# RWKV chunk inverse: products of (I+P) with [P-I, X], with the odd half of the pairs in the neighbouring column quarter and another PSUM bank

## The chip, the cores and the metric

The kernel runs on one core of one Trainium2 chip. The metric is device time in microseconds. Everything is float32.

## The reference, cut to what matters

One encoder layer over 1024 + 512 tokens of width 1024: RMSNorm, one projection into an RWKV-7 group (8 heads of 64, two directions) and an HGRN2 group, output projection, a mixture of 32 experts, a final norm. The change touches only the RWKV scan:

```python
def step(S, inp):
    r_t, w_t, k_t, v_t, kk_t, b_t = inp
    sa = jnp.einsum('dbhvk,dbhk->dbhv', S, -kk_t)
    S = S * w_t[..., None, :] + sa[..., None] * b_t[..., None, :] + v_t[..., None] * k_t[..., None, :]
    y_t = jnp.einsum('dbhvk,dbhk->dbhv', S, r_t)
    return S, y_t
```

The kernel computes it in chunks of 32 tokens. Inside a chunk the tokens depend on each other through a strictly triangular 32x32 matrix M, one for each head and direction, so 16 of them in each chunk. The chunk needs X = (I-M)^-1 = (I+M)(I+M^2)(I+M^4)(I+M^8)(I+M^16).

## The kernel before, in words

The stage is `mix_rwkv_project_hgrn`. It goes over 48 chunks (50 turns of the loop, since the work on a chunk is spread over three turns: `a = c+2`, `b = c+1`, `c`). Between the pieces of the scan, TensorE computes the HGRN columns of the input projection (`project`, L1202: 54 units of 8 matmuls of 128x512, shared out as 8 or 9 a turn). All orders are written out by hand: each engine has its own loop over the same turns and waits on marks (`Marks`) that other engines set.

The 16 matrices of a chunk lie as 4 partition quarters (`quad[q]`, 32 partitions each) times 4 pairs (`j`). TensorE works here on tiles: a matmul with 32 rows and 32 columns uses the part of the array given by the partition quarter that it reads (row quarter) and the one that it writes (column quarter). A float32 matmul shows as two records in the trace, so 16 matmuls are 32 records. In the text a block is such a set of 16 matmuls:

- right, L1246: the right-hand side from `sm` and `vz`, then L1250 from the state; mark R.
- I2 (`power(ps_b, ..., 2)`, L1231).
- solve, L1259 (X applied to `rs`), then L1262, the output from the state; mark UO.
- scores, L1221, then one projection matmul.
- grow, L1271 and L1275; mark MO.
- I3 (L1231), two projection matmuls, I0 (L1229), three projection matmuls (two in the later turns), I4 (L1234), I1 (L1231). L1231 is one line for I1, I2 and I3.

In L1229, L1231, L1234 and L1259 the matmul of quarter q reads quarter q and writes quarter q, for all pairs, so a block uses four tiles of the array, four times each. L1246 also uses four. L1250 and L1262 (`by_turn`) use eight tiles, each of which has 64 rows and 32 columns, and L1275 has four of that same shape.

VectorE's `grow` (L1439 to L1443) follows each I block: add P X to X, copy the new P out of PSUM (L1441), transpose it as the next stationary operand `pw` (L1443). The first transpose is L1544, the first X (M + I) is L1545, the last add into `xt` is L1556. Before L1544 in each turn VectorE does `grown` (L1536, waits for MO) and `state` (L1539); `masked` (L1431) makes `sm` from the scores. `scans` (L1456 to L1470) and `scaled` are for HGRN. `ps_a` (chunk a) and `ps_b` (chunk b) are one PSUM bank each.

## Time and profile before

| | us |
|---|---|
| median of 3 runs | 2321.32 (2316.4 to 2321.55) |
| profiled execution, its own time | 2317.24 |
| its span | 2315.7 |
| this stage's steady part, 508 to 1211 | 703.00 |

The span is the time between the first and the last record of the profiled execution. The stage is one of several that follow one another; the norm and the RWKV projection lie ahead of it, the HGRN scan, the output projection and the experts behind it. In a timeline row the first number is the start in us from the span's start, the second the time from the first start to the last end of the merged records, then engine, line, operation, operands, shape, count. "Idle before" stands in brackets. Since matmuls are pipelined, the time that a block costs TensorE is read from its start to the next block's start, not from the second number.

### The profile page before, as it was taken

To read this page: it belongs to the slowest core of one execution; us is meant where nothing else is said; L and a number is where in the kernel's file an instruction comes from. 1 tells how busy PE (TensorE), PEld (TensorE's weight loads), DVE (VectorE), ACT (ScalarE), POOL (GpSimd) and SP (SyncE) were. 2 spreads that over 40 slices of the span, in tenths; PEclk is the share of its full clock that TensorE was granted. 3 is DMA by queue.
4 is the path that set the end of the run, shared out by engine and by line. 5 is a ranking of instruction groups with operands and counts; after the bars stand their busy time and mean duration, and the time that the engine had idled before them with its cause. 6 is when DMAs were issued, how large, how long until landed. Compare 5 with 4: busy or idle time off the path is not lost. (4 is left out here: it accounts for less than half of the span.)

```text
span 2315.7 us, 64509 instructions
## 1 busy us (share of the span) xinstructions
PE 2215.1 (96%) x28004; PEld 1453.8 (63%) x28004; DVE 1032.3 (45%) x2221; ACT 717.5 (31%) x1446; POOL 407.9 (18%) x506
## 2 busy tenths in 40 slices
PE   7999999999999999999997999998999999999996
PEld 4444445445555555555556766756888888888884
DVE  3336767833654654644656765655211111111114
ACT  4224545623454543543642322222000000000003
POOL 1012222310000000000002120013524333233231
PEclk9999999999999999999998999998999999999998
DMA  4103444443333333333338754262999999999997
GB/s 144 37 23 128 153 147 137 167 113 93 94 105 88 91 103 94 94 104 89 84 107 258 233 169 132 97 236 70 363 381 335 357 364 328 354 357 335 353 335 293
DMA packets 359966, 436.66 MB, mean 189 GB/s; under 512 B 164994, under 2 KB 296198, under 8 KB 351536
## 3 DMA queue, kind: packets, MB, share of 16 engines
q1 hardware_dynamic: 343232, 397.94, 50.5%
q0 software_dynamic: 14384, 35.19, 6.0%
q8 instruction: 192, 3.15, 0.6%
q10 hardware_dynamic: 2112, 0.01, 0.1%
q14 instruction: 46, 0.38, 0.1%
HBM read 329.84 MB, written 104.50 MB: 188 GB/s over the span
## 5 line engine op out<-in xcount | busy, mean ns | idle before, releaser
L1202 PE MATMUL h_pp<-hT,r_wcol 128*128 128x512 f32 x832 | 414.0, 620 | 3.3 <-ACT h_iraw L1317 3.3
L2925 PEld LDWEIGHTS e_ps_gu<-e_xT,e_wu 128*128 128x128 f32 x2048 | 233.6, 192 | 14.3 <-issue 14.3
L2925 PE MATMUL e_ps_gu<-e_xT,e_wg 128*128 128x128 f32 x2048 | 235.2, 276 | 0.0
L2925 PE MATMUL e_ps_gu<-e_xT,e_wu 128*128 128x128 f32 x2048 | 233.8, 275 | 0.0
L2925 PEld LDWEIGHTS e_ps_gu<-e_xT,e_wg 128*128 128x128 f32 x2048 | 232.5, 193 | 0.4 <-DVE e_xT L3043 0.4
L2934 PE MATMUL e_ps_y<-e_wd,e_hid 128*128 128x512 f32 x512 | 225.1, 592 | 0.8 <-DVE e_hid L3097 0.8
L1202 PEld LDWEIGHTS h_pp<-hT,r_wcol 128*128 128x128 f32 x832 | 141.8, 190 | 124.6 <-issue 109.4
L522 PE MATMUL h_pp<-hT,r_wcol 128*128 128x512 f32 x480 | 209.1, 593 | 1.3 <-DVE hT L794 1.3
L3050 DVE TENSOR_SCALAR e_y<-e_ps_y,e_row 128x512 f32<-128x512 f32 x31 | 23.3, 750 | 325.0 <-PE e_ps_y L2934 325.0
L2934 PEld LDWEIGHTS e_ps_y<-e_wd,e_hid 128*128 128x128 f32 x512 | 94.8, 190 | 108.8 <-issue 107.1
L522 PEld LDWEIGHTS h_pp<-hT,r_wcol 128*128 128x128 f32 x480 | 90.3, 191 | 109.7 <-issue 108.1
L2989 ACT ACTIVATE e_silu<-e_ps_gu 128x512 f32<-128x512 f32 x31 | 18.5, 597 | 410.3 <-PE e_ps_gu L2925 396.6
L2718 POOL DMA_INDIRECT e_x<-h,e_idx x128 | 124.6, 973 | 55.6 <-issue 29.5
L2286 PE MATMUL o_ps_out<-o_wout,y 128*128 128x512 f32 x288 | 129.4, 594 | 4.0 <-DVE y L2520 4.0
L2041 POOL MEMSET g_mask<- 128x256 f32 x1 | 0.3, 312 | 735.3 <-POOLq L1058 735.3
L1379 ACT ACTIVATE m_v<-m_ps_x 32x256 f32<-32x256 f32 x192 | 71.9, 374 | 147.0 <-PE m_ps_x L1262 145.3
L3057 DVE TENSOR_TENSOR e_hid<-e_ps_gu,e_silu 128x512 f32<-128x512 f32 x31 | 21.4, 691 | 204.7 <-PE e_ps_gu L2925 204.7
L776 POOL TENSOR_TENSOR r_spans<-r_spans 128x512 f32<-128x512 f32 x24 | 42.0, 1768 | 370.6 <-DVE r_spans L866 370.6
L522 PE MATMUL r_pp<-hT,r_wcol 128*128 128x512 f32 x240 | 105.4, 592 | 0.0
L2286 PEld LDWEIGHTS o_ps_out<-o_wout,y 128*128 128x128 f32 x288 | 52.2, 190 | 58.6 <-issue 58.6
L522 PEld LDWEIGHTS r_pp<-hT,r_wcol 128*128 128x128 f32 x240 | 45.4, 190 | 56.4 <-issue 56.4
L2985 ACT ACTIVATE e_y<-e_ps_y,e_row 128x512 f32<-128x512 f32 x31 | 21.3, 688 | 184.0 <-PE e_ps_y L2934 184.0
(428 smaller groups left out, 3398.3 us busy)
## 6 DMA issues: line engine op xcount, KB each, us to landing
e_wg<-in_moe_w_gate_dram SPq DMA_DIRECT2D x32, 2048.0 KB
e_wu<-in_moe_w_up_dram SPq DMA_DIRECT2D x32, 2048.0 KB
e_wd<-in_moe_w_down_dram SPq DMA_DIRECT2D x32, 2048.0 KB
r_wcol<-in_w_in_dram SPq DMA_DIRECT2D x35, 512.0 KB, 4.7
ar<-r_ar SPq DMA_DIRECT2D x24, 512.0 KB, 2.7
kb<-r_kb SPq DMA_DIRECT2D x24, 512.0 KB, 2.8
m_ar<-ar SPq DMA_DIRECT2D x48, 256.0 KB, 4.7
m_kb<-kb SPq DMA_DIRECT2D x48, 256.0 KB, 3.5
```

The costliest lines, as they stand in the source:

```text
L522: last = nc.tensor.matmul(pp[k % SPANS][:], wcol[q][:, c], self.hT[:, c, s * SPAN:(s + 1) * SPAN], start=c == 0, stop=c == KT - 1)
L776: nc.gpsimd.tensor_tensor(gx[d][:], gi[d][:], sg[d][:], ALU.subtract).then_inc(*pool_aux.inc(f"gx{d}"))
L1202: last = nc.tensor.matmul(pp[n % 2][:], wcol[(k + 2) % 3][:, c], self.hT[:, c, span(s)], start=c == 0, stop=c == KT - 1)
L1379: last = nc.scalar.activation(out, ps_ru[quad[q]], ACT.Copy)
L2286: last = nc.tensor.matmul(ps_out[:, h * SPAN:(h + 1) * SPAN], y[:, k, tile(FINISHED[n])], wout[:, k, h * SPAN:(h + 1) * SPAN], start=k == ...
L2718: self.nc.gpsimd.indirect_dma_start(self.e_x[u][:, g], None, self.h2.rearrange("t (q e) -> (t q) e", q=4), bass.IndirectOffsetOnAxis(ap=se ...
L2925: last = nc.tensor.matmul(ps[:, q * P:(q + 1) * P], w[u][:, c, q * P:(q + 1) * P], xT[u][:, c * P:(c + 1) * P], start=c == 0, stop=c == KT ...
L2934: last = nc.tensor.matmul(ps_y[:, n * 512:(n + 1) * 512], hid[u][:, q * P:(q + 1) * P], wd[u][:, q, n * 512:(n + 1) * 512], start=q == 0, ...
L2985: return nc.scalar.activation(y[u][:, 0:512], ps_y[:, 0:512], ACT.Copy, scale=gate[u])
L2989: made = nc.scalar.activation(silu[:], ps_g, ACT.Silu)
L3050: return nc.vector.tensor_scalar(y[u][:, 512:], ps_y[:, 512:], gate[u], None, ALU.mult)
L3057: made = nc.vector.tensor_tensor(hid[u][:], ps_u, silu[:], ALU.mult)
```

## The change

X is kept in PSUM's own sum: with (I+P) as the stationary operand and [P-I, X] as the moving one, a single matmul gives [P^2-I, X+PX]. The first block multiplies M with [M, I]. VectorE adds I (or 2I) to the left half and writes that into a spare part of the same PSUM tile (S), copies both halves into `px` (N), and transposes the spare part out of PSUM (turn). The separate add into X goes, as do X0 and `xt`. For pairs 2 and 3 the matmuls write the neighbouring column quarter (`q ^ 1`) and, as `ps_p` is two banks, the other bank; pairs go in the order 0, 2, 1, 3. The columns of `ps_ru` for w = 1 are exchanged in the same way. As chunks a and b now share `ps_p`, I0, I4 and I1 get one wait more, and one projection matmul stands between I4 and I1.

```diff
-            m0 = sb("m_m0", [P, PAIRS, CH])
+            m0 = sb("m_m0", [P, PAIRS, 2 * CH])
-            xt = [sb(f"m_xt{u}", [P, PAIRS, CH]) for u in range(2)]
-            eye = sb("m_eye", [P, CH])
+            eyes = sb("m_eyes", [P, 3 * CH])
-            ps_a = psum("a", [P, PAIRS, P])
-            ps_b = psum("b", [P, PAIRS, P])
+            ps_p = psum("p", [P, PAIRS, 2 * P])
+            ps_a = ps_b = ps_p
...
-                        nc.gpsimd.affine_select(out=eye[r], in_=eye[r], compare_op=ALU.not_equal, fill=1.0, base=0,
-                                                pattern=[[-1, CH]], channel_multiplier=1).then_inc(filled, 1)
+                        for part, value in enumerate((-1.0, 1.0, 2.0)):
+                            e = eyes[r, part * CH:(part + 1) * CH]
+                            nc.gpsimd.affine_select(out=e, in_=e, compare_op=ALU.not_equal, fill=value, base=0,
+                                                    pattern=[[-1, CH]], channel_multiplier=1).then_inc(filled, 1)
...
                     def power(ps, u, i):
-                        for j in range(PAIRS):
-                            for q in quad:
-                                if i == 0:
-                                    last = nc.tensor.matmul(ps[q, j, 0:CH], pw[u][q, j], m0[q, j], start=True, stop=True)
-                                elif i < 4:
-                                    last = nc.tensor.matmul(ps[q, j, 0:2 * CH], pw[u][q, j], px[u][q, j], start=True,
-                                                            stop=True)
+                        for j in (0, 2, 1, 3):
+                            for q in range(P // CH):
+                                r, o = quad[q], quad[q ^ (j // 2)]
+                                if i < 4:
+                                    last = nc.tensor.matmul(ps[o, j, 0:2 * CH], pw[u][r, j], px[u][r, j] if i else m0[r, j],
+                                                            start=True, stop=True)
                                 else:
-                                    last = nc.tensor.matmul(ps[q, j, CH:2 * CH], pw[u][q, j], px[u][q, j, CH:],
+                                    last = nc.tensor.matmul(ps[o, j, CH:2 * CH], pw[u][r, j], px[u][r, j, CH:],
                                                             start=True, stop=True)
...
-                            nc.tensor.matmul(ps_ru[quad[2 * k + d], w, i], sm[c % RING][r, g, 0:CH], vz[c % 2][r, g],
+                            nc.tensor.matmul(ps_ru[quad[(2 * k + d) ^ w], w, i], sm[c % RING][r, g, 0:CH], vz[c % 2][r, g],
...
-                        for j in range(PAIRS):
-                            for q in quad:
-                                nc.tensor.matmul(ps_ru[q, j % 2, j // 2], xt[c % 2][q, j], rs[q, j], start=True, stop=True)
+                        for j in (0, 2, 1, 3):
+                            for q in range(P // CH):
+                                r = quad[q ^ (j // 2)]
+                                nc.tensor.matmul(ps_ru[quad[q], j // 2, j % 2], px[c % 2][r, j, CH:], rs[r, j], start=True,
+                                                 stop=True)
...
                         if has_a:
-                            self.waits(eng, dve_a.at("P0", a))
+                            self.waits(eng, dve_a.at("P0", a), dve_b.at("turn4", b) if has_b else None)
                             power(ps_a, a % 2, 0).then_inc(*pe_a.inc("I0"))
-                        project(it, 6, 9)
+                        project(it, 6, 8)
                         if has_b:
-                            self.waits(eng, dve_b.at("turn4", b))
+                            self.waits(eng, dve_b.at("turn4", b), dve_a.at("turn1", a) if has_a else None)
                             power(ps_b, b % 2, 4).then_inc(*pe_b.inc("I4"))
+                        project(it, 8, 9)
                         if has_a:
-                            self.waits(eng, dve_a.at("turn1", a))
+                            self.waits(eng, dve_a.at("turn1", a), dve_b.at("X4", b) if has_b else None)
                             power(ps_a, a % 2, 1).then_inc(*pe_a.inc("I1"))
...
                     def grow(marks, ps, b, i):
 
                         u = b % 2
-                        if i > 1:
-                            nc.vector.tensor_tensor(px[u][:, :, CH:], px[u][:, :, CH:], ps[:, :, CH:2 * CH], ALU.add
-                                                    ).then_inc(*marks.inc(f"X{i - 1}"))
-                        nc.vector.tensor_copy(px[u][:, :, 0:CH], ps[:, :, 0:CH]).then_inc(*marks.inc(f"P{i}"))
-                        self.waits(eng, marks.at(f"P{i}", b))
-                        nc.vector.transpose(pw[u][:], px[u][:, :, 0:CH]).then_inc(*marks.inc(f"turn{i}"))
+                        each = lambda lo, n: eyes[:, lo * CH:(lo + n) * CH].unsqueeze(1).broadcast_to((P, PAIRS, n * CH))
+                        spare = ps[:, :, 2 * CH:3 * CH]
+                        nc.vector.tensor_tensor(spare, ps[:, :, 0:CH], each(1 if i == 1 else 2, 1), ALU.add
+                                                ).then_inc(*marks.inc(f"S{i}"))
+                        if i == 1:
+                            nc.vector.tensor_tensor(px[u][:], ps[:, :, 0:2 * CH], each(0, 2), ALU.add
+                                                    ).then_inc(*marks.inc(f"N{i}"))
+                        elif i < 4:
+                            nc.vector.tensor_copy(px[u][:], ps[:, :, 0:2 * CH]).then_inc(*marks.inc(f"N{i}"))
+                        else:
+                            nc.vector.tensor_copy(px[u][:, :, CH:], ps[:, :, CH:2 * CH]).then_inc(*marks.inc(f"N{i}"))
+                        self.waits(eng, marks.at(f"S{i}", b))
+                        nc.vector.transpose(pw[u][:], spare).then_inc(*marks.inc(f"turn{i}"))
...
-                            nc.vector.transpose(pw[a % 2][:], m0[:]).then_inc(*dve_a.inc("P0"))
-                            nc.vector.tensor_tensor(px[a % 2][:, :, CH:], m0[:],
-                                                    eye[:].unsqueeze(1).broadcast_to((P, PAIRS, CH)), ALU.add
-                                                    ).then_inc(*dve_a.inc("X0"))
+                            nc.vector.transpose(pw[a % 2][:], m0[:, :, 0:CH]).then_inc(*dve_a.inc("P0"))
...
-                            nc.vector.tensor_tensor(xt[b % 2][:], px[b % 2][:, :, CH:], ps_b[:, :, CH:2 * CH], ALU.add
-                                                    ).then_inc(*dve_b.inc("X4"))
+                            nc.vector.tensor_copy(px[b % 2][:, :, CH:], ps_b[:, :, CH:2 * CH]).then_inc(*dve_b.inc("X4"))
```

ScalarE's copies into `m0` and `rs` only take the pairs in another order.

## Rows read from the trace of the kernel before

**Rows 1.** The page, part 1: busy time, share of the span, instructions of each engine.
```profile
PE 2215.1 (96%) x28004; PEld 1453.8 (63%) x28004; DVE 1032.3 (45%) x2221; ACT 717.5 (31%) x1446; POOL 407.9 (18%) x506
```

**Rows 2.** Windows, steady part: length; PE, PEld, DVE, ACT, POOL busy; PEclk; DMA; GB/s.
```profile
508.00:1211.00 703.00, 685.57 (x18878) 401.27 (x18872) 368.51 (x1042) 323.19 (x738) 0.00 (x0) 1.00 0.37 94
```

**Rows 3.** Lines of the steady part, two groups of one shape: count, busy, mean, idle before.
```profile
L1275 PE MATMUL m_ps_x<-m_v,m_sm 64*32 64x64 f32 x1504 | 33.1, 220 | 0.6 <-issue 0.6
...
L1262 PE MATMUL m_ps_x<-m_state,m_ar 64*32 64x64 f32 x1504 | 22.9, 222 | 1.8 <-issue 1.8
```

**Rows 4.** Timeline of one turn, TensorE's matmul rows: start, extent, engine, line, count.
```profile
803.25 0.67 PE L1275 MATMUL m_ps_x<-m_v,m_sm 64*32 64x64 f32 x32
...
803.86 0.65 PE L1231 MATMUL m_ps_b<-m_px,m_pw 32*32 32x64 f32 x32
...
804.44 1.98 PE L1202 MATMUL h_pp<-hT,r_wcol 128*128 128x512 f32 x4
...
806.35 0.45 PE L1229 MATMUL m_ps_a<-m_m,m_pw 32*32 32x32 f32 x32
...
806.74 2.84 PE L1202 MATMUL h_pp<-hT,r_wcol 128*128 128x512 f32 x6
...
809.51 0.45 PE L1234 MATMUL m_ps_b<-m_px,m_pw 32*32 32x32 f32 x32
...
809.78 0.65 PE L1231 MATMUL m_ps_a<-m_px,m_pw 32*32 32x64 f32 x31
...
810.24 0.64 PE L1246 MATMUL m_ps_x<-m_v,m_sm 32*32 32x64 f32 x30
...
810.80 0.45 PE L1250 MATMUL m_ps_x<-m_state,m_ar 64*32 64x64 f32 x32
...
813.10 0.65 PE L1231 MATMUL m_ps_b<-m_px,m_pw 32*32 32x64 f32 x32
...
813.57 0.62 PE L1259 MATMUL m_ps_x<-m_rs,m_xt 32*32 32x64 f32 x32
...
814.13 0.45 PE L1262 MATMUL m_ps_x<-m_state,m_ar 64*32 64x64 f32 x32
...
814.51 0.81 PE L1221 MATMUL m_ps_s<-m_ar,m_kb 64*64 64x128 f32 x7
```

**Rows 5.** The same turn, VectorE's rows between MO and the end.
```profile
804.01 0.69 DVE L1536 TENSOR_TENSOR m_grown<-m_ps_x,m_state 128x512 f32<-128x512 f32 x1 [0.83 <-PE m_ps_x L1275]
...
805.34 0.30 DVE L1544 STREAM_TRANSPOSE m_pw<-m_m 128x128 f32<-128x128 f32 x1
...
805.57 0.25 DVE L1545 TENSOR_TENSOR m_px<-m_m,m_eye 128x128 f32<-128x128 f32 x1
805.74 0.28 DVE L1439 TENSOR_TENSOR m_px<-m_px,m_ps_b 128x128 f32<-128x128 f32 x1
805.93 0.28 DVE L1441 COPY m_px<-m_ps_b 128x128 f32<-128x128 f32 x1
806.25 0.31 DVE L1443 STREAM_TRANSPOSE m_pw<-m_px 128x128 f32<-128x128 f32 x1
...
807.21 0.31 DVE L1443 STREAM_TRANSPOSE m_pw<-m_px 128x128 f32<-128x128 f32 x1
...
810.04 0.29 DVE L1556 TENSOR_TENSOR m_xt<-m_px,m_ps_b 128x128 f32<-128x128 f32 x1 [2.52 <-PE m_ps_b L1234]
```

**Rows 6.** Waits of the steady part: engine, line, what was waited for, total us, times, longest.
```profile
PE m_ps_s L1221 <- issue: 3.6, 6, 1.2
```

**Rows 7.** DMA queues of the steady part: packets, MB, share of 16 engines' time.
```profile
q8 instruction: 149, 2.44, 1.5%
```

**Rows 8.** Timeline, a turn with an HGRN scan in it, VectorE's L1536.
```profile
1163.19 0.69 DVE L1536 TENSOR_TENSOR m_grown<-m_ps_x,m_state 128x512 f32<-128x512 f32 x1 [0.36 <-PE m_ps_x L1275]
```

**Rows 9.** Start of the stage: the last constant on GpSimd, the first mask on VectorE.
```profile
487.28 0.69 POOL L1076 TENSOR_SCALAR_AFFINE_SELECT m_mask<-m_mask 32x32 f32<-32x32 f32 x4
...
490.36 0.80 DVE L1431 TENSOR_TENSOR m_sm<-m_ps_s,m_mask 128x256 f32<-128x256 f32 x2 [1.44 <-PE m_ps_s L1221]
```

More of the change, by code:

```diff
@@ L967, in mix_rwkv_project_hgrn @@
             lb0, lb1, lb, olb, nolb = (sb("h_" + n, [P, 2, PAIRS]) for n in ("lb0", "lb1", "lb", "olb", "nolb"))
-            sb("h_below", [P, 92])
+            sb("h_below", [P, 156])
             self.first = kq_first, k3_first, k2_first = self.first_chunk(sb("h_first", [P, 3 * D + SPAN]))
@@ L993, in mix_rwkv_project_hgrn @@
             act_c = Marks(self.sem("m_act_back"), "r u O")
-            dve_a = Marks(self.sem("m_dve_first"), "mask0 mask1 P0 X0 P1 turn1 X1 P2 turn2")
-            dve_b = Marks(self.sem("m_dve_last"), "X2 P3 turn3 X3 P4 turn4 X4")
+            dve_a = Marks(self.sem("m_dve_first"), "mask0 mask1 P0 S1 N1 turn1 S2 N2 turn2")
+            dve_b = Marks(self.sem("m_dve_last"), "S3 N3 turn3 S4 N4 turn4 X4")
             dve_c = Marks(self.sem("m_dve_back"), "grown state")
@@ L1015, in mix_rwkv_project_hgrn @@
             dve_q = Marks(self.sem("h_dve_q"), "Q0 K0 Q1 K1 Q2 K2")
-            FILLED = 3 + 5 * (P // CH) + 3
+            FILLED = 3 + 7 * (P // CH) + 3
             V_LOADS = 16 * 8
@@ L1061, in _ @@
                     nc.gpsimd.memset(mask[:], 1.0).then_inc(filled, 1)
-                    nc.gpsimd.memset(eye[:], 0.0).then_inc(filled, 1)
+                    nc.gpsimd.memset(eyes[:], 0.0).then_inc(filled, 1)
                     nc.gpsimd.memset(state[0][:], 0.0).then_inc(filled, 1)
@@ L1249, in right @@
                             g = 4 * d + 2 * i + w
-                            last = nc.tensor.matmul(ps_ru[quad[2 * (h ^ w) + d], w, i], ar[c % RING][heads[h], g, 0:CH],
+                            last = nc.tensor.matmul(ps_ru[quad[(2 * (h ^ w) + d) ^ w], w, i], ar[c % RING][heads[h], g, 0:CH],
                                                     state[c % 2][heads[h], g], start=False, stop=True,
@@ L1369, in _ @@
                             self.waits(eng, pe_c.at("R", c))
-                            nc.scalar.activation(rs[:].rearrange("p (i w) v -> p w i v", w=2), ps_ru, ACT.Copy
+                            nc.scalar.activation(rs[:].rearrange("p (w i) v -> p w i v", w=2), ps_ru, ACT.Copy
                                                  ).then_inc(*act_c.inc("r"))
@@ L1388, in _ @@
                                 d = q % 2
-                                last = nc.scalar.activation(m0[quad[q]], sm[a % RING][quad[q], d * PAIRS:(d + 1) * PAIRS, 0:CH],
-                                                            ACT.Copy)
+                                last = nc.scalar.activation(
+                                    m0[quad[q], :, 0:CH].rearrange("p (w i) n -> p w i n", w=2),
+                                    sm[a % RING][quad[q], d * PAIRS:(d + 1) * PAIRS, 0:CH].rearrange("p (i w) n -> p w i n", w=2),
+                                    ACT.Copy)
                             last.then_inc(*act_a.inc("m0"))
@@ L1426, in _ @@
                     eng.wait_ge(filled, FILLED)
-                    eng.wait_ge(cleared, 1 + 2 * RING)
+                    nc.vector.tensor_copy(m0[:, :, CH:], eyes[:, CH:2 * CH].unsqueeze(1).broadcast_to((P, PAIRS, CH))
+                                          ).then_inc(cleared, 1)
+                    eng.wait_ge(cleared, 2 + 2 * RING)
                     by_dir = lambda ap: ap.rearrange("p (d i) n -> p d i n", d=2)
```

## The prediction

> **What bounds the kernel now.** I read the page first. TensorE is busy for 96% of the span [rows 1]; the other engines for less than half. A reader should then leave the whole-kernel share alone and ask the stage. The windows view gives, for the 703.0 us between 508 and 1211 us, a busy TensorE of 685.6 us at a granted clock of 1.00 (2.4 GHz), VectorE 368.5 and ScalarE 323.2 [rows 2]. So TensorE's order sets the pace of the 48 chunks, one turn of the loop each, and what matters is how long each block holds TensorE, plus the places where it would have to wait. The kernel's last stage, where the chain of waits ends, isn't touched; what this stage gives back is passed on whole, because all engines leave it together.
>
> The timeline of one turn shows how regular it is [rows 4]. From start to next start: I3 0.58 (803.86 to 804.44), two projection matmuls 1.91, I0 0.38, three projection matmuls 2.77 (these are six records), I4 0.27, I1 0.46, L1246 0.56, I2 0.47, solve 0.56, L1262 0.38, L1275 0.61. The reader is to compare blocks with the same count of records (32) and the same 64 moving columns: L1275 0.61 against L1262 0.38. These two even have the same tile shape, 64 rows by 32 columns. Over the whole steady part it is 33.1 against 22.9 us busy [rows 3], 10.2 us in 47 blocks, 0.22 us a block. The code says what differs: L1275 goes round four tiles of the array, L1262 round eight. Per tile, then, a block is eight passes in a row with four tiles, four passes with eight tiles. I2, which is followed by a block of the same shape with no switch, gives the length of a pass: 0.47/8 = 0.058 us.
>
> **The change part by part.**
>
> *The eight-tile blocks.* By the code, L1246, I0 to I4 and solve now go round eight tiles (quarter q to q, then q to its neighbour, in another bank), as L1262 does today. No row shows eight tiles of 32 rows; the nearest are the 64-row ones. Bounds for one block of 64 columns: nothing saved (if 32-row tiles in one row quarter don't overlap), 0.23 us saved (0.61 - 0.38). I take what lies close to the upper end, because L1262 has four tiles in each row half and they overlap: I2 goes from 0.47 to 0.47 - 4 x 0.056 = 0.25; L1246 from 0.56 and solve from 0.56 to 0.37, a shade under L1262's 0.38, since both are followed by a change of tile shape as it is. Saved on TensorE: I2 0.22, L1246 0.19, solve 0.19, together 0.60 us a turn. I3 would save 0.20 as well, but see the next step.
>
> *I3 and the new wait of I0.* In front of I0 stands now "turn4 of chunk b". Today VectorE, released by MO, does L1536 at 804.01, the state, the transpose L1544 at 805.34, X0 at 805.57, the add 805.74, the copy 805.93 and the transpose of turn4 at 806.25 to 806.56 [rows 5]; I0 starts at 806.35 without waiting for the last one. In the changed order X0 falls away: S4 starts at 805.57, N4 at 805.76 (the present spacing of 0.19), turn4 at about 805.96, since S4 (0.29 long, like the present adds) ends at 805.86, and it ends at about 806.28. With some 0.06 us for the signal I0 starts at 806.34, where it starts today. TensorE would be there at 806.35 - 0.20 = 806.15. So I3's gain turns into a wait of about 0.2 us for VectorE, and MO to I0 stays as long as it is. The forms "add from PSUM into PSUM" and "transpose out of PSUM" have no row. Bounds: as their SBUF twins (0.25 to 0.31), or later by the 0.13 us that today's dependent pair shows over independent ones (0.32 against 0.19 between starts) plus as much again for the PSUM side, which puts I0 0.2 us later; I take 0.0 to 0.05 later. Behind the waiting I0 are the projection matmuls, I4 and I1, thus everything; ScalarE's next unit only follows.
>
> *I0 with 64 instead of 32 columns.* Four tiles at 32 columns cost 0.38 with the shape switch; eight tiles at 64 columns with the switch cost 0.38 (L1262). Nothing.
>
> *I4, the projection between, I1.* Today three projections, I4 and I1 are 2.77 + 0.27 + 0.46 = 3.50 us. Then: two projections 1.91, I4 with eight tiles and a shape switch behind it 0.35 (today I0, with as many columns and four tiles, has 0.38; an eight-tile block of 64 columns has 0.38 as well, so little is won by more tiles on a block of 32), one projection 1.06 (as 2.77 - 1.91 is 0.86 and two switches bring 0.20), I1 0.25. That is 3.57: 0.07 us lost to the two extra switches, in place of 0.21 won on I1. Bounds 0.0 to 0.15 lost.
>
> *The waits of I4 and I1.* turn1 starts at 807.21 and ends 1.17 us after I0's start [rows 5]. N1 is wider (256 elements, about 0.40 by L1431's 0.80 for two of that width [rows 9], 0.12 more than now), and I4 comes 2.3 us after I0: 0.9 us to spare. X4 starts 0.53 us after I4's start and lasts 0.29; I1 comes 1.4 us after I4's start: 0.5 to spare. Both waits are free while VectorE isn't behind.
>
> *VectorE in all.* An instruction goes (X0), three copies grow by about 0.12, so its load is as it was, 52% of the stage [rows 2]. But in the turns with an HGRN scan its work is near the edge: L1536 had waited for MO for 0.36 us only [rows 8], against 0.83 in the other turn [rows 5]. The path from I1 through the scans to L1536 gets 0.6 us shorter on TensorE and not on VectorE, so in about 8 turns (one for each of the 8 scans) L1536 comes some 0.25 us late, 0.6 - 0.36: 2 us.
>
> *Constants.* Eight more small selects on GpSimd at 0.2 us: the last ends at 487.97 today, its first reader starts at 490.36 [rows 9]. 1.6 us fit into 2.4. The VectorE copy of I into `m0` lies there too. Nothing.
>
> *Instruction loading.* TensorE's instructions come in 149 loads in this part [rows 7], one per 4.7 us, and some blocks of short matmuls show holes put down to "issue", in L1221 3.6 us in 6 holes, the longest 1.2 [rows 6]; that is the largest of seven such groups, so all of them stay under 25 us. The count of instructions stays, the blocks get shorter, so a hole can grow by what the blocks before it lost (up to 0.4 us), while the projection put between I4 and I1 gives the loading more time. I take +1 us; from -3 to +10.
>
> *The sum.* -0.60 + 0.07 = -0.53 us a turn; 48 turns make -25.4 us; +2 for the scans and +1 for the loading leave -22.4 us. From the profiled execution (span 2315.7, own time 2317.2) that gives 2294.8. The median of the three runs is 4.1 us above the profiled execution, so in the terms of that median the time is 2321.3 - 22.4 = 2299.
>
> *A rule that speaks against it.* L1250 and L1262 have four column tiles in each row half, and their 32 records take 0.38 us, against 0.61 for four tiles [rows 3, 4]. The Trainium skill (TensorE: Matmul & The Clock Gate, Part 3: Packing small matmuls) says that a weight load overlaps matmuls in flight only when the row group differs. By that rule the tiles q to q and q to its neighbour, which read the same row quarter, would not overlap, and the change would cost time (first rival). The trace disagrees for 64-row tiles; no row shows 32-row ones.
>
> **The rivals.**
>
> 1. *Eight tiles don't overlap (slower).* Place: every I block, L1246, solve. Then nothing is saved, I0 pays for its wider columns (0.58 as I3, against 0.38: +0.20), and the split of I4 and I1 costs 1.91 + 0.41 + 1.06 + 0.47 = 3.85 against 3.50: +0.35. 0.55 x 48 = +26 us: 2348. It decides when a block wins less than 0.55/5 = 0.11 us, half of what I take, since five blocks count (I3's gain is hidden). For it: no row with 32-row tiles. Against it: L1262. Chance 0.06.
> 2. *VectorE's chain to turn4 is longer, or instruction holes grow.* Each 0.1 us on the chain from MO to turn4 is 4.8 us. At +0.2 us it takes 9.6 us, and +8 us of holes come to much the same: 2308. For it: two forms without a row, holes that already lie in the short blocks. Against it: all PSUM forms of this size last 0.28 to 0.29, like the SBUF ones plus 0.03. Chance 0.25.
> 3. *turn4 doesn't hold I0 up.* If N4 overlapped more, I3's 0.2 us would come as well: 9.6 us more, 2289. Against it: L1544 starts 1.33 us after L1536 [rows 5], both wide instructions before it stay, and three instructions follow it. Chance 0.10.
> 4. *No difference.* A combination in which the late turns with scans and the holes take most of it: 2318. Chance 0.07.
>
> **How the numbers follow.** The forecast has 0.52. Its own range is 2293 to 2305. The range for 8 in 10 takes in rival 2 and rival 3 with their bounds: 2285 to 2312. About 0.3% (7 us) is what a measurement can tell from no change. Faster by more: 0.52 + 0.25 + 0.10 = 0.87; within it 0.07 (rival 4); slower 0.06 (rival 1).
>
> **What would show it.** After the change L1246, L1259 and the I blocks with 64 columns should have extents near 0.45, as L1262 has now, not 0.65, and the rows for four against eight tiles in the lines view should be equal; TensorE should show a wait for VectorE's transpose out of PSUM ahead of I0, about 0.2 us, nearly every turn; MO to I0 should stay 2.64 to 2.7 us; a turn with 16 projection records should take about 0.53 us less, so that the stage ends some 22 us earlier; I4 and I1 should start without waiting. It is wrong if blocks keep 0.65 (rival 1), if I0 comes later after MO than today (rival 2), or if the holes put down to "issue" grow past 25 us.

## The result, and the profile after

The changed kernel takes 2336.9 us (median of 8 runs, 2332.4 to 2345.6), the kernel before 2321.4 us in the same series (8 runs): ratio 1.0074, 95% interval 1.0061 to 1.0086. It is 15.5 us slower where 22 us faster was forecast. The time is lost in the stage forecast to gain: the first matmul of the next stage starts at 1239.68 us in place of 1223.28, and what follows is as long as before (1093.2 against 1092.4 us).

The page of the changed kernel, part 1, and the windows view of the same 703 us as in [rows 2] (same columns):

```profile
PE 2207.0 (95%) x28004; PEld 1419.6 (61%) x28004; DVE 1033.4 (44%) x2222; ACT 718.5 (31%) x1446; POOL 409.0 (18%) x514
```

```profile
508.00:1211.00 703.00, 660.27 (x18386) 358.38 (x18376) 364.16 (x1024) 320.34 (x730) 0.00 (x0) 1.00 0.35 91
```

Three things are to be seen here. The clock is the same (1.00), TensorE is busy for 25 us less than in [rows 2], and yet it gets through 492 records fewer in the same time. So it is idle longer, and what fills the idle time is the question. The timeline of one turn of the changed kernel, TensorE's matmul rows (start, extent, then as in [rows 4]):

```profile
900.44 0.67 PE L1277 MATMUL m_ps_x<-m_v,m_sm 64*32 64x64 f32 x32
901.04 0.45 PE L1231 MATMUL m_ps_p<-m_px,m_pw 32*32 32x64 f32 x32
901.42 1.98 PE L1203 MATMUL h_pp<-hT,r_wcol 128*128 128x512 f32 x4
903.57 0.46 PE L1231 MATMUL m_ps_p<-m_m,m_pw 32*32 32x64 f32 x32 [0.16 <-DVE m_pw L1457]
903.96 1.98 PE L1203 MATMUL h_pp<-hT,r_wcol 128*128 128x512 f32 x4
905.87 0.35 PE L1234 MATMUL m_ps_p<-m_px,m_pw 32*32 32x32 f32 x32
906.15 1.12 PE L1203 MATMUL h_pp<-hT,r_wcol 128*128 128x512 f32 x2
907.21 0.45 PE L1231 MATMUL m_ps_p<-m_px,m_pw 32*32 32x64 f32 x32
907.53 0.53 PE L1246 MATMUL m_ps_x<-m_v,m_sm 32*32 32x64 f32 x32
908.00 0.45 PE L1250 MATMUL m_ps_x<-m_state,m_ar 64*32 64x64 f32 x32
908.38 1.98 PE L1203 MATMUL h_pp<-hT,r_wcol 128*128 128x512 f32 x4
910.29 0.45 PE L1231 MATMUL m_ps_p<-m_px,m_pw 32*32 32x64 f32 x32
910.56 0.57 PE L1260 MATMUL m_ps_x<-m_rs,m_px 32*32 32x64 f32 x30
911.80 0.29 PE L1260 MATMUL m_ps_x<-m_rs,m_px 32*32 32x64 f32 x2 [0.67 <-issue]
912.02 0.46 PE L1264 MATMUL m_ps_x<-m_state,m_ar 64*32 64x64 f32 x32
```

Against [rows 4]: I3 takes 0.38 (901.04 to 901.42) in place of 0.58, I2 0.27 in place of 0.47. L1246, right behind I1, takes 0.47, and the solve, right behind I2, is broken off after 30 of its 32 records; in a turn without such a gap it takes 0.52:

```profile
818.32 0.59 PE L1260 MATMUL m_ps_x<-m_rs,m_px 32*32 32x64 f32 x32
818.84 0.31 PE L1264 MATMUL m_ps_x<-m_state,m_ar 64*32 64x64 f32 x6
820.58 0.44 PE L1264 MATMUL m_ps_x<-m_state,m_ar 64*32 64x64 f32 x26 [1.43 <-issue]
```

Such gaps, put down to "issue" (TensorE waited for nothing that the profile shows), are where the time went. The waits view of the changed kernel, 508 to 1230 us (columns as in [rows 6]), the largest groups of the short blocks' matmuls, and the wait of I0 (first and sixth row):

```profile
PEld m_ps_p L1231 <- DVE m_pw L1558: 36.6, 39, 1.3
...
PE m_ps_s L1222 <- issue: 8.4, 9, 1.6
...
PE m_ps_x L1264 <- issue: 7.5, 8, 1.4
...
PE m_ps_x L1277 <- issue: 6.6, 7, 1.2
...
PE m_ps_x L1260 <- issue: 4.5, 6, 1.2
...
PE m_ps_p L1231 <- DVE m_pw L1457: 3.9, 20, 0.5
PE m_ps_x L1246 <- issue: 3.7, 6, 0.9
```

All "issue" rows of the short blocks' matmuls add up to 35.9 us, before to 16.3 us; L1222 has 8.4 us against 3.6 [rows 6]. Where I write "gaps" below I count them from the records themselves: two consecutive matmul records of one short block that start more than 0.18 us apart, between 508 and 1225 us. Before there are 27, together 18 us, after 60, together 50 us. With the gaps taken out, a turn is some 0.3 us shorter than before: 15 us gained, 32 us given away.

What the gaps have in common can be read from the order of the records. Each matmul record stands for two TensorE instructions (a weight load and a matmul), and in both kernels every gap lies at the same place modulo 256 TensorE instructions, so some 127 records from the next possible one. The queue that brings in instructions shows the same step (the changed kernel, 508 to 1230 us, columns as in [rows 7]):

```profile
q8 instruction: 149, 2.44, 1.4%
```

2.44 MB in 149 loads is 16 KB a load, and some 38,000 TensorE instructions in 149 loads are 256 a load. That the gaps lie in short blocks says little by itself, since only 8 or 9 of the some 150 steps between 508 and 1225 us fall in a projection; one of these, at 523.5 us in the changed kernel, shows a pause too (0.88 us between two starts where 0.43 or 0.53 is usual). How deep a step falls in a row of short blocks counts: of those in the first short block behind a projection 13 of 57 have a gap, in the second 22 of 41, in the third 18 of 30, deeper 10 of 11 (before: 6 of 48, 7 of 34, 9 of 32, 8 of 28; counted with a gap between two blocks taken in).

The gaps can also be set against the times of these loads. The load ahead of the gap shown above (TensorE stands from 910.92 to 911.80) runs from 909.30 to 910.43, and the next one begins at 913.41. The DMA view of the changed kernel for 909.2 to 910.5 and for 913.3 to 914.5 us has one load each, for the time between them none:

```profile
q8 instruction: 1, 0.02, 5.4%
...
q8 instruction: 1, 0.02, 5.0%
```

So the gap ends 1.37 us after the end of a load. It is the same nearly everywhere: 57 of the 60 gaps of the changed kernel and all 27 of the one before end 1.1 to 1.7 us after the end of a load (median 1.4), and the other three are among the shortest (0.22 to 0.26 us). Of the short blocks' records in general only some 14% start that far behind a load. Between each two of the 256-instruction steps exactly one load ends at least 1.15 us ahead of the second step, in both kernels, and after a gap the next load never starts earlier than 1.04 us behind it. From load to load it is at least 3.2 us. A gap is thus TensorE standing at the end of its 256 instructions until the next ones are in.

### The profile page after: what moved, and what is told of

Same layout as the page of the kernel before. It is cut to its first block and busy times, and to the rows that moved or that the text cites. A ratio compares the mean times of both kernels' runs of the same rounds, so it can differ in the third digit from the quotient of the medians.

```text
span 2332.9 us, 64667 instructions
## 1 busy us (share of the span) xinstructions
PE 2207.0 (95%) x28004; PEld 1419.6 (61%) x28004; DVE 1033.4 (44%) x2222; ACT 718.5 (31%) x1446; POOL 409.0 (18%) x514
## 3 DMA queue, kind: packets, MB, share of 16 engines
q8 instruction: 192, 3.15, 0.6%
## 5 line engine op out<-in xcount | busy, mean ns | idle before, releaser
L1203 PE MATMUL h_pp<-hT,r_wcol 128*128 128x512 f32 x832 | 426.3, 626 | 3.7 <-ACT h_iraw L1320 3.3
L522 PE MATMUL h_pp<-hT,r_wcol 128*128 128x512 f32 x480 | 211.1, 597 | 1.3 <-DVE hT L794 1.3
L1447 DVE TENSOR_TENSOR m_ps_p<-m_ps_p,m_eyes 128x128 f32<-128x128 f32 x192 | 55.9, 291 | 150.7 <-PE m_ps_p L1231 150.7
L1231 PEld LDWEIGHTS m_ps_p<-m_px,m_pw 32*32 32x32 f32 x4608 | 42.9, 104 | 78.6 <-issue 74.0
```

What stands on the lines that cost most here:

```text
L522: last = nc.tensor.matmul(pp[k % SPANS][:], wcol[q][:, c], self.hT[:, c, s * SPAN:(s + 1) * SPAN], start=c == 0, stop=c == KT - 1)
L1203: last = nc.tensor.matmul(pp[n % 2][:], wcol[(k + 2) % 3][:, c], self.hT[:, c, span(s)], start=c == 0, stop=c == KT - 1)
L1231: last = nc.tensor.matmul(ps[o, j, 0:2 * CH], pw[u][r, j], px[u][r, j] if i else m0[r, j], start=True, stop=True)
L1447: nc.vector.tensor_tensor(spare, ps[:, :, 0:CH], each(1 if i == 1 else 2, 1), ALU.add).then_inc(*marks.inc(f"S{i}"))
```

## The experiments

Each ran beside the kernel before (medians 2320.9 to 2322.5 us in the five series). Labels that begin with a_ are edits of the changed kernel, with b_ of the one before. "Gaps" are counted as above.

| run | median, us | ratio to before, interval | gaps, us (count) |
|---|---|---|---|
| changed kernel | 2336.9 | 1.0074 [1.0061, 1.0086] | 50 (60) |
| a_four | 2351.8 | 1.0124 [1.0100, 1.0149] | 32 (45) |
| b_split | 2332.2 | 1.0044 [1.0027, 1.0061] | 18 (28) |
| b_twice | 2340.8 | 1.0088 [1.0066, 1.0110] | 26 (39) |
| a_less | 2312.2 | 0.9961 [0.9943, 0.9980] | 49 (69) |
| a_later | 2346.2 | 1.0107 [1.0087, 1.0127] | 53 (53) |
| a_spread | 2342.0 | 1.0080 [1.0063, 1.0097] | 48 (59) |
| b_spread | 2329.2 | 1.0037 [1.0022, 1.0051] | 13 (19) |
| a_even | 2376.3 | 1.0223 [1.0201, 1.0245] | 60 (62) |
| b_waits | 2334.0 | 1.0068 [1.0043, 1.0094] | 25 (38) |
| a_order | 2332.4 | 1.0048 [1.0026, 1.0070] | 48 (62) |
| a_swap | 2338.6 | 1.0076 [1.0048, 1.0104] | 45 (61) |
| a_both | 2332.8 | 1.0046 [1.0023, 1.0069] | 43 (48) |
| b_pad_d | 2531.3 | 1.0911 [1.0882, 1.0940] | |
| b_pad_p | 2412.3 | 1.0397 [1.0379, 1.0414] | |
| a_reord | 2345.5 | 1.0106 [1.0088, 1.0123] | 48 (49) |
| a_cut | 3213.5 | 1.3842 [1.3819, 1.3865] | |
| a_prune | 2308.2 | 0.9950 [0.9932, 0.9968] | 29 (39) |
| b_prune | 2317.0 | 0.9979 [0.9963, 0.9994] | 25 (38) |

**One part of the change at a time.**

a_four puts all blocks back on four tiles, with the new algebra, waits and order kept:

```diff
-                                r, o = quad[q], quad[q ^ (j // 2)]
+                                r, o = quad[q], quad[q]
```

> The changed kernel with its algebra, its shared two banks, its waits and its order, but every block back on four tiles (quarter q writes quarter q). TensorE needs about 0.2 us more for each block of 64 columns of 32-row tiles. Theory L (TensorE's instructions arrive in loads of 256, and where the work of 256 instructions is shorter than a load takes, TensorE stands still; so shorter blocks turn into holes): most of the longer blocks goes into the holes, 2337 +- 8 us, with holes inside the short blocks down from 50 us to under 25. Theory T (the eight-tile blocks do save their time, and the loss comes from waits and switches of tile shape): 0.6 to 0.9 us more a turn, 2366 to 2380 us, holes as in the changed kernel.

The eight tiles are worth 15 us, though 18 us more of gaps come with them. They aren't the loss; everything else in the change together costs 30 us.

b_split only puts the projection between I4 and I1, in the kernel before:

```diff
-                        project(it, 6, 9)
+                        project(it, 6, 8)
 ...
+                        project(it, 8, 9)
```

> The kernel before with one thing of the change: one projection matmul moved from in front of I4 to between I4 and I1. Two switches of tile shape more a turn; by the blocks' lengths I4 to L1246 goes from 3.50 to 3.83 us. Theory T: +0.33 us x 48 = +16 us, 2337 us, the whole loss. Theory L: the row of short blocks I4, I1, L1246, L1250 is broken up, so its holes (about 4 us in I1) go, +8 to +13 us, 2329 to 2334 us, and it is not the cause of more holes.

It costs 10 us, and the gaps stay at 18: all of it is TensorE's own time. I4, now in front of a projection, takes 0.38 in place of 0.27, and the projections on both sides have their changes of shape.

**Is it the number of instructions, or the density?**

b_twice issues I0 twice (`power(ps_a, a % 2, 0)` once more), 64 instructions a turn:

> The kernel before with the 16 matmuls of I0 issued twice in a row (same result): 64 TensorE instructions more a turn, and 0.25 us more of TensorE time. Theory T: +12 us, 2333 us. Theory L: a quarter of a load more a turn, and a load's period is 4.7 us, so up to 1.2 us a turn: +25 to +50 us, 2346 to 2371 us, with holes up from 18 us to over 30.

a_less leaves out L1277's matmuls, and with them the part of the output that comes from within the chunk:

> The changed kernel without the 16 matmuls of L1277 (the part of the output that comes from within the chunk is left out, the state is right): 64 TensorE instructions less a turn and 0.60 us less of TensorE time. Theory T: -29 us, 2308 us, holes as in the changed kernel. Theory L: holes shrink by half as well (50 to 25 us or less), 2278 to 2292 us.

Both came out between or beside the theories. b_twice costs 19 us: I0 takes 0.68 us in place of 0.38, some 14 us in all, and the gaps grow by 8. a_less gains 25 us, a little less than the blocks' own duration (0.60 us a turn, 29 in all), with the gaps unchanged: a mere rate of loading per turn doesn't set them.

a_later (`project(it, 4, 7)` in front of I0, `project(it, 7, 8)` behind it), a_spread, b_spread (`project(it, 0, 2)`, I2, `project(it, 2, 3)`) and a_even (one projection at each of those places) move projections about:

> The changed kernel with three projection matmuls in front of I0 and one between I0 and I4, in place of two and two. It tests the step on turn4: in the changed kernel the two projections before I0 and I3 take 2.12 us where 1.92 us would do without the wait. Theory T (the stage is the sum of TensorE's work and waits): 0.2 us x 48 turns = 10 us less, 2327 us, range 2323 to 2331. Rival W (the wait only moves: I4 now waits for turn1, whose chain of sum, copy and transpose ends some 1.3 us after I0 while one projection gives 1.07): no gain, 2335 to 2341. Rival H (what is not waited is lost again as gaps inside the short blocks): gaps rise from 50 us to 56 or more and the time stays 2333 to 2340.

> The changed kernel with one of the three projection matmuls in front of I2 moved behind I2, so that the run of four short blocks I2, solve, output from state, scores is cut after the first. No work is added. Theory T (only TensorE's own durations count): I2 takes 0.38 us in place of 0.27 since it is now followed by a projection, the solve 0.38 in place of 0.52: nothing, 2334 to 2340 us, gaps inside the short blocks stay at 50 us. Theory D (the gaps come where 256 TensorE instructions are used up in less than the 3.3 us that lie at least between two instruction loads, so in the dense runs of short blocks): gaps fall from 50 us to 20 to 38, time 2310 to 2328 us.

> The kernel before with the same move (one projection from in front of I2 to behind it), so the same edit at the lower density of four-tile blocks. Theory T: I2 0.58 in place of 0.47 us, solve as it is: up to 5 us slower, 2321 to 2327 us, gaps stay at 18 us. Theory D: gaps fall from 18 us to 5 to 12, time 2310 to 2321 us.

> The changed kernel with its nine projections spread as evenly as the waits allow: one, I2, one, solve and output from state, one, scores, one, the two growing blocks and I3, three, I0, one, I4, one, I1 and the two blocks of R. Theory T: three more switches between projection and short block at 0.12 us each, less 0.14 for the solve and 0.2 for the wait of I0: 2337 + 48 x 0.02 = 2338 us, 2330 to 2343, gaps 50 us. Theory D: gaps fall to 8 to 25 us: 2296 to 2316 us, which would be below the kernel before.

Theory D's forecast, fewer gaps with the dense runs broken up, fell: a_spread has as many, at other places, and a_even, meant to be the best, is the slowest of these. (In the later turns a turn has eight projections, not nine, and the missing one is the first, so that in a_even I2 follows L1250 directly in 31 turns.) Its premise, that a gap is a wait for a load, stands by the times above; in a_spread too 55 of 59 gaps end 1.1 to 1.7 us behind one. What moving a single projection doesn't do is to make the stretches of 256 instructions long enough: I2, the solve, the output from the state and the scores are 128 records and take 2.2 us by the rows above, against 3.2 us from load to load. a_later is more telling: the wait of I0 goes, yet I4's wait for turn1 becomes tight, and the kernel is 9 us slower. One thing did follow the prediction, a block's length. In the timeline of a_spread the solve stands behind a projection:

```profile
901.34 1.12 PE L1203 MATMUL h_pp<-hT,r_wcol 128*128 128x512 f32 x2
902.40 0.45 PE L1260 MATMUL m_ps_x<-m_rs,m_px 32*32 32x64 f32 x32
902.78 0.41 PE L1264 MATMUL m_ps_x<-m_state,m_ar 64*32 64x64 f32 x18
```

It takes 0.38 us (902.40 to 902.78) and not the 0.52 of 818.32: the solve is fast behind a projection, and slower behind an eight-tile block of its own shape. I1 and L1246 take 0.32 + 0.47, I2 and the solve 0.27 + 0.52, 0.79 us for each pair. My reading, which no run shows by itself, is that TensorE's sequencer, which hands the instructions to the array, fills a queue while the array does long work, and that the block before has used it up.

**Waits.** This led to theory Q: the sequencer is near its limit, and waits cost it time.

b_waits adds to b_split the changed kernel's waits of I4 (turn1) and I1 (X4), which nothing needs there:

```diff
-                            self.waits(eng, dve_a.at("turn1", a))
+                            self.waits(eng, dve_a.at("turn1", a), dve_b.at("X4", b) if has_b else None)
```

> The kernel before in the split order (two projections, I4, one projection, I1; alone that took 2332 us, with gaps of 18 us inside the short blocks) with two waits added that nothing in it needs: I4 also waits for turn1 and I1 also waits for X4, as in the changed kernel. Both are met before TensorE gets there (turn1 stands some 1.3 us after I0 begins and I4 comes after 2.3; X4 stands some 0.7 us after I4 and I1 comes after 1.3). Theory T (a wait that is met in time is free): 2329 to 2335 us, gaps 16 to 21 us. Theory Q (TensorE's sequencer runs ahead of the array and so asks for its next 256 instructions early; a wait that is met only just in time holds the sequencer though the array is busy, so that its lead is gone when the dense blocks come): gaps 28 to 45 us, time 2341 to 2356 us.

a_order moves VectorE's L1550 and L1553 behind the transpose of turn4; a_swap puts I1 behind `right(c)` of the next turn; a_both does both:

> The changed kernel with VectorE's order in a turn changed: transpose of M, then sum, copy and transpose 4 (which I0 waits for), and only then the two state operations of 0.69 us each. TensorE's order is as it was. Theory T: I0 no longer waits for turn4, 0.2 us x 48 = 10 us less, 2327 us, range 2322 to 2331, gaps 50 us. Theory Q: the same 10 us, and the sequencer is no longer held at I0: gaps fall to 30 to 42 us, 2308 to 2320 us. Rival H (what is not waited is lost again as gaps, as with the later I0): 2333 to 2345 us.

> The changed kernel with I1 behind the two blocks of R of the next turn in place of in front of them, so that I1's wait for X4 has 0.9 us more room, and I2's for turn2 as much less (it keeps some 0.6). Theory T: the block after I4's projection is now L1246 and takes 0.38 in place of 0.46, the rest as it was: 2333 to 2338 us, gaps 50 us. Theory Q: the sequencer enters the blocks of R with a lead, gaps fall to 25 to 42 us and the time to 2310 to 2329 us. If the wait for turn2 counts instead, gaps stay or grow and the time is 2337 to 2350.

> The changed kernel with both edits: VectorE's order with the state operations last, and I1 behind the blocks of R. Theory T: 2324 to 2329 us. Theory Q: both holds of the sequencer gone, gaps 15 to 30 us, 2290 to 2310 us, below the kernel before. Rival H: 2333 us or more.

b_waits: gaps up from b_split's 18 to 25 us, time only 2 us up in the medians (6 by the two ratios to the kernel before, whose intervals overlap); theory Q had asked for more. a_order gains 4.5 us of the 10 that its wait was worth (I0 behind two projections now 1.91 us nearly every turn, the wait for VectorE down to 0.2 us in all), a_swap and a_both nothing further. So moving the waits to where they are met earlier helps little. The number of waits had not been tried by itself, so the next pair adds nothing but instructions that wait for what has long been there, at two places of the kernel before:

```diff
+                        for _ in range(64):
+                            eng.wait_ge(filled, FILLED)
```

(The program packs two such waits into one instruction, hence 32.)

> The kernel before with 32 more TensorE instructions in every turn that give the array no work (waits on a semaphore that has long had its value), between the solve and the output from state, in the middle of the run of short blocks. Theory A (what counts is the number of instructions to be brought in: 4% more, wherever they stand): gaps inside short blocks grow from 18 us to 19 to 24, and the time by 1 to 7 us, as in the twin kernel with the same instructions between two projections. Theory S (in a run of short blocks the sequencer has no lead over the array, so that each instruction there costs the array its own time): 5 to 25 us more than the twin. Time 2322 to 2328 by A, 2330 to 2350 by S.

> The twin: the same 32 idle instructions per turn between the second and third projection behind I0, while the array works on projections for 2 us. Theory A: as the other, 2322 to 2328 us, gaps 19 to 24 us. Theory S: hidden behind the projections, 2320 to 2325 us, gaps 16 to 21 us.

Both theories were far too low, by a factor of about ten: it is 210 and 91 us. The timeline of b_pad_d, solve and output from state:

```profile
903.06 0.62 PE L1259 MATMUL m_ps_x<-m_rs,m_xt 32*32 32x64 f32 x32
906.77 0.46 PE L1264 MATMUL m_ps_x<-m_state,m_ar 64*32 64x64 f32 x32 [3.09 <-issue]
907.17 1.10 PE L1221 MATMUL m_ps_s<-m_ar,m_kb 64*64 64x128 f32 x32
```

From start to start 3.71 us, in [rows 4] 0.56 (813.57 to 814.13): 3.15 us for 32 instructions, 0.098 us each, though each wait had been met 400 us earlier. (The block behind the pause, with nothing queued, then takes 0.40 us, against 0.38, and 0.39 in most of the other turns at full clock: an empty queue alone slows a block of 64-row tiles by no more than that. Whether it is what slows the 32-row ones to 0.52 is thus not shown.) And b_pad_p, between the second and third projection behind I0:

```profile
897.86 1.98 PE L1202 MATMUL h_pp<-hT,r_wcol 128*128 128x512 f32 x4
901.27 1.10 PE L1202 MATMUL h_pp<-hT,r_wcol 128*128 128x512 f32 x2 [1.43 <-issue]
```

Here 3.41 us, where four records take 1.71 (2.77 for six less 1.06 for two): 1.7 us of the 3.15 show, and 1.45 us were hidden behind the projections. So that is how far the sequencer can be ahead of the array there. Theory S was right in kind: the same instructions cost 119 us more in the run of short blocks.

How the 210 us come about can be read in the windows view of b_pad_d (columns as in [rows 2]):

```profile
903.00:907.00 4.00, 0.91 (x80) 0.78 (x72) 1.20 (x5) 0.00 (x0) 0.00 (x0) 1.00 0.36 104
508.00:1400.00 892.00, 740.07 (x18543) 433.64 (x18541) 366.21 (x1031) 323.57 (x731) 0.00 (x0) 0.90 0.28 73
```

The pause of 3.15 us stands in a stretch of full clock, so it is no effect of the clock; 48 of them are 151 us. The rest goes with a granted clock of 0.90 over the stage: in 24 of 47 turns the block behind the pause takes 0.61 us in place of 0.39 (at 888.1 us, for one, with a granted clock of 0.51). In b_pad_p, where the pause is 1.7 us, the clock stays at 1.00, and 48 x 1.7 = 82 us of its 91 are the pauses.

a_reord and a_cut were to put all 256-instruction steps behind projections, by padding a turn with some 210 idle instructions (a_reord is the same order without them):

> The changed kernel with VectorE's state operations last in a turn (2332 us so far) and its projections spread: one behind I1, one in front of I2, one between I2 and the solve, one behind the scores, two behind I3, two behind I0, one behind I4, so that no run has more than four short blocks. Control for the next kernel. Gaps have not followed the spread so far (48 us with one moved): theory T 2326 to 2336 us, gaps 42 to 52 us.

> The same order with idle instructions (36 to 58 behind the projections that stand after I1, I2, the scores and I3) that make a turn exactly 4 x 256 instructions long, so that from the tenth turn or so every 256-instruction boundary, at which the gaps have been seen, lies directly behind a projection and none inside a run of short blocks; before it was 3.15 boundaries a turn, wherever they fell. Theory P (a gap is what is left of a fixed stall at the boundary after the work queued before it; behind 1.06 us of projection most of it is covered): gaps nearly gone, 0 to 12 us, time 2285 to 2305 us. Rival R (a load of 256 instructions takes at least 3.3 us, whatever lies at its boundary): three of the four stretches are 2.7 to 3.3 us long and each is drawn out to 3.3 to 4.3 us, some 1.5 us a turn, time 2380 to 2420 us.

At 0.1 us each these cost some 20 us a turn and buried the question; theories P and R stay untested. a_reord, at 2345.5 us with gaps of 48, is slower than the 2326 to 2336 expected, and its gaps are as expected. The windows view of a_cut also shows what such pauses do to the clock:

```profile
700.00:1900.00 1200.00, 710.10 (x14024) 365.63 (x14026) 289.15 (x789) 247.04 (x552) 0.00 (x0) 0.72 0.16 42
```

**Fewer waits.** a_prune is a_order without the waits of TensorE that others imply, seven instructions a turn; b_prune is the kernel before without three:

```diff
-                            self.waits(eng, dve_a.at("P0", a), dve_b.at("turn4", b) if has_b else None)
+                            self.waits(eng, dve_b.at("turn4", b) if has_b else dve_a.at("P0", a))
 ...
-                        self.waits(eng, dve_c.ago("state", c, 1), act_c.ago("O", c, 1),
-                                   (v_loaded[c % 2], (c // 2 + 1) * V_LOADS), dve_a.at("mask1", c))
+                        self.waits(eng, act_c.ago("O", c, 1), (v_loaded[c % 2], (c // 2 + 1) * V_LOADS),
+                                   dve_c.ago("state", c, 1) if c > CHUNKS - 3 else None)
```

> The changed kernel with VectorE's state operations last (2332 us) and without TensorE's redundant waits: of every set of waits those are left out that an earlier or the kept wait already implies by the order of work on VectorE or ScalarE (I0 waits for turn4 alone, I4 for turn1, I1 for X4, the solve for r, growing for u, the scores for their two loads, R for its load and O). That is 7 wait instructions a turn less on TensorE, 2 left; each of them was met in time. Theory T (a met wait is free): 2328 to 2337 us. Theory Q (each costs TensorE's sequencer about 0.1 us, as the 32 idle ones did: 3.19 us in place of none in the gap they made): up to 7 x 0.1 x 48 = 34 us less, a part of it hidden behind projections: 2298 to 2320 us, gaps 20 to 40 us.

> The kernel before without its redundant waits (3 wait instructions a turn less of 6). Theory T: 2318 to 2324 us. Theory Q: up to 3 x 0.1 x 48 = 14 us less: 2307 to 2317 us, gaps 8 to 16 us.

a_prune takes 2308.2 us, 24 us less than a_order (in another series), and is 0.5% faster than the kernel before. It is the only complete variant of the changed kernel that is faster; theory T (a met wait is free) falls. The matmuls and their order are a_order's. The waits view of a_prune, 508 to 1205 us:

```profile
PE m_ps_x L1264 <- issue: 5.0, 6, 1.3
...
PE m_ps_s L1222 <- issue: 3.5, 7, 0.8
PE m_ps_p L1231 <- issue: 3.4, 3, 1.2
PE m_ps_x L1277 <- issue: 3.0, 6, 1.0
PE m_ps_x L1273 <- issue: 2.4, 4, 1.1
PE m_ps_x L1260 <- issue: 2.3, 4, 1.1
```

The "issue" groups are down to some 20 us from 35, the gaps from 48 to 29. b_prune gains 5 us (interval of the ratio 0.9963 to 0.9994) although its gaps grow, from 18 to 25 us.

## Why the prediction was wrong

**Eight tiles overlap: right.** I2 0.27 (0.25 predicted), I3 0.38. The first rival, which had the time nearest to the measured one (2348), had the wrong mechanism: 32-row tiles overlap as 64-row ones do. The rule weighed there, of the Trainium skill (TensorE: Matmul & The Clock Gate, Part 3: Packing small matmuls), says that a weight load overlaps matmuls in flight only where the row group differs. What it would do here, nothing saved, doesn't show in this trace: I2's 32 records, with two tiles in each row quarter, take 0.27 us in place of 0.47.

**L1246 and the solve at 0.37: the third step that failed, a wrong size.** They take 0.47 and 0.52, and the solve 0.38 where a projection stands before it (a_spread). That is 0.25 us a turn, 12 us in all. I had read L1250 and L1262 (0.38) as the array's pace for eight tiles anywhere; both stood behind slower blocks.

**MO to I0, the wait for turn4: right.** VectorE's rows of the changed kernel's turn shown above:

```profile
901.19 0.69 DVE L1550 TENSOR_TENSOR m_grown<-m_ps_x,m_state 128x512 f32<-128x512 f32 x1 [0.93 <-PE m_ps_x L1277]
901.92 0.69 DVE L1553 TENSOR_TENSOR m_state<-m_grown,m_decay 128x512 f32<-128x512 f32 x1
902.53 0.30 DVE L1558 STREAM_TRANSPOSE m_pw<-m_m 128x128 f32<-128x128 f32 x1
902.75 0.27 DVE L1447 TENSOR_TENSOR m_ps_p<-m_ps_p,m_eyes 128x128 f32<-128x128 f32 x1
902.93 0.27 DVE L1455 COPY m_px<-m_ps_p 128x128 f32<-128x128 f32 x1
903.13 0.30 DVE L1457 STREAM_TRANSPOSE m_pw<-m_ps_p 128x128 f32<-128x128 f32 x1
```

L1277's start to I0's is 3.13 us (900.44 to 903.57), before 3.10 (803.25 to 806.35) [rows 4]. The two forms without a row cost what their SBUF twins do. TensorE waits about 0.2 us, as said: from the start of the two projections to I0 it is 2.12 us in the median turn, before 1.91. In four turns out of five it is put down to VectorE on the weight load (36.6 us in 39 times, most of it beside the array's work).

**I0 with 64 columns, the split: right, the split with luck.** I0 takes 0.39. From the next start behind I0 to L1246 it is 3.57 us (903.96 to 907.53), 3.57 predicted, but I4 takes 0.28 where 0.35 was predicted and I1 0.32 where 0.25 was; the two errors cancel.

**The late turns with scans, +2 us: not seen by themselves.** In the turn at 1162 us L1550 waits for MO for 1.48 us, where [rows 8] has 0.36, and in five turns of the changed kernel it doesn't wait at all, against two before; no run isolates what that costs.

**The waits of I4 and I1, "both waits are free": the second step that failed, a term put at nothing.** They are met in time, as predicted (turn1 ends at 904.98, 0.9 us ahead of I4, and X4 0.5 us ahead of I1), but the program makes an instruction of its own of each second wait. The trace of the changed kernel has 817 of these on TensorE, the one before 676: 141 or three more a turn (I0, I4, I1). I asked only when a wait is met, never what it costs the sequencer to look. The Trainium skill (Perfetto Trace Analysis, Identifying Dependency Chains) says that an instruction that waits for several engines can get such instructions in front of it; the count agrees. It gives them no price; here it is 0.098 us each.

**Instruction loading, +1 us, at most +10: the step that failed, and the largest error in the sum.** The gaps grew by 32 us. The prediction's own warning sign ("if the holes put down to 'issue' grow past 25 us") is what the waits view shows. The reasoning was that a hole that is there grows at most by what the blocks before it lost, up to 0.4 us. The mean gap did grow by no more than that, from 0.67 to 0.83 us. What the reasoning left out is new gaps: 60 in place of 27, as more of the stretches of 256 instructions are now worked off before the next load is in. The sequencer's lead counts for this too: where it is well ahead of the array, idle waits were half hidden (b_pad_p), and where it isn't, they showed in full (b_pad_d). From b_split's 18 us of gaps the two added waits lead to 25 (b_waits), the rest of the change on four tiles, with I0's third wait, to 32 (a_four), and the eight-tile blocks to 50. The Trainium skill (Runtime: NRT & Kernel Launch, Instruction fetch mechanics) says that stepping from one 256-instruction block to the next is mostly hidden, because the sequencer hands out instructions more slowly than they come in. Most of the 150 steps of the kernel before show no gap, which agrees; in dense runs of short matmuls it doesn't hold, 60 of the changed kernel's 148 steps show one.

In numbers, from 2321.4: the array's time -15 us (-25 predicted), the gaps +32 (+1 predicted), together +17; measured +15.5. Of the 32, 18 come with the eight-tile blocks alone (a_four against the changed kernel). How much is the waits' can only be bounded: at b_waits' price 2 to 7 us, at a_prune's (24 us for seven, 0.07 us each) 10 us. That removing seven waits wins 24 us while adding two costs 2 is not explained; a_order, from which a_prune starts, has less lead than the kernel before, and in b_prune too three waits are worth only 5 us.

**What stays open.** That TensorE waits at a 256-instruction step for a load is read from the times, in all the traces; no run changed the loads themselves. When the next load is asked for, and so how a wait instruction or a shorter block makes it late, the traces don't tell. Nor was the share of I0's wider columns in the gaps isolated. One way of taking I4's and I1's waits away altogether, buffers of their own for chunks a and b, wasn't tried: the eight-tile blocks as written here use two PSUM banks for a chunk, and the stage uses all eight.

## What to carry to other kernels

Where TensorE runs long rows of small matmuls, the supply of instructions is a resource like the array: here 0.1 us for each extra wait instruction, and at least 3.2 us between two loads of 256 instructions. Before you make such blocks faster, compare the time of each 128 records in a row with that, and take out waits that the order of another engine's work already implies; the change was worth having only then (2308 against 2317 us with both kernels pruned, where the first also has a_order's edit and lost seven waits a turn, the second three). And a chance of 0.87 on "faster" was too high with an unexplained class of idle time already in the rows.

## What the runs showed of the hardware

A wait that has long been met costs TensorE's sequencer 0.098 us an instruction (b_pad_d, 3.15 us for 32), hidden up to about 1.45 us behind two projections (b_pad_p). TensorE's instructions come in loads of 16 KB, 256 instructions, at least 3.2 us apart, and where TensorE is through with its own before, it stands until some 1.4 us after the end of the next load (27 gaps before, 60 after, 0.2 to 1.9 us each). An eight-tile block of 32 records takes 0.27 us behind a projection and in front of a block of its own shape (I2), 0.38 in front of a change of shape (I3), and 0.47 to 0.52 where an eight-tile block of its own shape stands before it and a change of shape behind it. With one pause of 3.15 us in each turn the granted clock of the stage was 0.90 in place of 1.00 (b_pad_d), with four of 2 to 6 us it was 0.72 (a_cut). VectorE adds from PSUM into PSUM in 0.27 to 0.30 us and transposes out of PSUM (128x128) in 0.30, as out of SBUF.
